# Weight copies issued up to three units ahead, and constant multiplications ahead of TensorE's waits, in a two-block transformer kernel

## The reference, cut to what matters

```python
def first_block(x, ...):              # 1040 tokens
    h = rms_norm(h_res, pre_mix_g); proj = h @ w_in            # q1 q2 k1 k2 v u
    o = diff_attention(q1, q2, k1, k2, v, lam)                 # causal, softmax(q1 k1) - lam softmax(q2 k2)
    y = s5_ssm(u, ...); y = y * sigmoid(gelu(y) @ w_glu + b)   # state space side
    h_res = h_res + rms_norm(concat(o, y) @ w_out)
    h = rms_norm(h_res); f = (silu(h @ w_gate) * (h @ w_up)) @ w_down    # width 2816
    return h_res + rms_norm(f)
def second_block(x, p, ...):
    proj = rms_norm(x) @ w_in                                  # retention q k v gate, RWKV columns
    mixed = concat(retention(...), rwkv7_mix(...))
    x = x + mixed @ w_o
    x = x + (silu(hf @ w_gate) * (hf @ w_up)) @ w_down         # hf = rms_norm(x)
    x = x + (p @ w_ple_up) * sigmoid(rms_norm(x) @ w_ple_gate)
    return rms_norm(x)
```

## Time and profile before

| what | value |
| --- | --- |
| median of 3 runs | 3360.91 us (3358.93 to 3362.32) |
| the profiled execution: its time | 3366.5 us |
| its span, first to last instruction | 3364.7 us |
| PE busy | 3066.1 us (91%) |
| PE weight loads / DVE / ACT / POOL busy | 71% / 45% / 36% / 36% |
| mean granted TensorE clock | 0.950 |

### The profile page before, as it was taken

One profiled execution on the slowest core, in us unless ns is written; L12 is line 12 of the kernel. 1 busy time (PEld: TensorE's weight loads), 2 busy tenths in 40 slices (PEclk: granted clock), 3 DMA queues, 4 the chain that ended last, 5 costly groups with the idle time before them and its releaser, 6 DMA issues.

```text
span 3364.7 us, 48162 instructions
## 1 busy us (share of the span) xinstructions
PE 3066.1 (91%) x19536; PEld 2383.2 (71%) x19536; DVE 1510.8 (45%) x2264; ACT 1225.0 (36%) x1969; POOL 1224.4 (36%) x698
## 2 busy tenths in 40 slices
PE   6997888899998889989999989998999988899997
PEld 4775656666776667777777767776777766788875
DVE  5835552444443441465565453435445554222233
ACT  3111134533433463334444345342444433322233
POOL 5811302232323323334444433424444422344432
PEclk9888789899999989999999999998999989999998
DMA  4344323222222444322222244332222222322231
GB/s 152 117 128 110 101 77 111 93 69 82 74 68 78 138 145 157 105 78 76 80 84 67 85 153 157 118 101 79 73 90 78 79 70 79 121 98 95 93 106 57
DMA packets 158029, 330.01 MB, mean 98 GB/s; under 512 B 34960, under 2 KB 74064, under 8 KB 157808
## 3 DMA queue, kind: packets, MB, share of 16 engines
q1 hardware_dynamic: 104000, 237.86, 22.7%
q10 hardware_dynamic: 53808, 89.07, 7.7%
HBM read 281.89 MB, written 44.97 MB: 97 GB/s over the span
## 4 chain that ended last, share of the span: by engine, by line
PE 77%; DVE 10%; ACT 4%; POOL 3%; issue 2%; DMA 2%; ACTq 1%; SPq 0%; DVEq 0%; POOLq 0%
PE ps L1953 31%; PE ps L1979 13%; PE ps L1991 12%; POOL w_lo L735 2%; PE ps L1804 2%; PE ps L1715 2%; PE ps L1685 1%; DVE acc_dense L2386 1%; PE ps L1725 1%; PE ps L1832 1%; DVE act_lo L2386 1%; ACT w_hi L846 1%; PE ps L2185 1%; DVE turn L2386 1%; PE ps L1892 1%
## 5 line engine op out<-in xcount | busy, mean ns | idle before, releaser
L735 POOL TENSOR_TENSOR w_lo<-w_raw,w_hi 128x1024 fp32r<-128x1024 f32 x408 | 995.1, 2451 | 1695.9 <-ACT w_hi L846 1692.3
L1953 PE MATMUL ps<-act_hi,w_hi 128*128 128x512 f32 x1696 | 700.4, 413 | 36.6 <-POOL w_lo L735 26.6
L1953 PE MATMUL ps<-act_hi,w_lo 128*128 128x512 f32 x1696 | 670.9, 396 | 0.0
L1953 PE MATMUL ps<-act_lo,w_hi 128*128 128x512 f32 x1696 | 670.4, 395 | 0.0
L1953 PEld LDWEIGHTS ps<-act_hi,w_hi 128*128 128x128 f32 x1696 | 323.9, 191 | 128.9 <-issue 48.5
L846 ACT ACTIVATE w_hi<-w_raw 128x1024 fp32r<-128x1024 f32 x378 | 387.1, 1052 | 70.1 <-issue 35.4
L1953 PEld LDWEIGHTS ps<-act_hi,w_lo 128*128 128x128 f32 x1696 | 323.4, 191 | 71.4
L1953 PEld LDWEIGHTS ps<-act_lo,w_hi 128*128 128x128 f32 x1696 | 324.4, 191 | 62.4 <-issue 1.4
L2386 DVE TENSOR_TENSOR acc_dense<-acc_dense,ps 128x512 f32<-128x512 f32 x352 | 241.9, 687 | 247.0 <-PE ps L1979 195.7
L1979 PE MATMUL ps<-w_hi,ffh_hi 128*128 128x512 f32 x704 | 294.0, 418 | 34.3 <-POOL w_lo L735 17.7
L1991 PE MATMUL ps<-w_hi,act_hi 128*128 128x512 f32 x640 | 257.4, 402 | 37.1 <-POOL w_lo L735 22.5
(11 more groups left out here) (380 smaller groups left out, 4346.7 us busy)
## 6 DMA issues: line engine op xcount, KB each, us to landing
w_raw<-weights SPq DMA_DIRECT2D x408, 512.0 KB, 3.5
rw<-rw_t ACTq DMA_DIRECT2D x24, 256.0 KB, 2.4
rw<-lora_t ACTq DMA_DIRECT2D x24, 256.0 KB, 2.0
row<-x ACTq DMA_DIRECT2D x8, 512.0 KB, 4.0
row_dense<-x ACTq DMA_DIRECT2D x8, 512.0 KB, 5.6
row_mix<-res ACTq DMA_DIRECT2D x8, 512.0 KB, 7.5
res<-row_mix ACTq DMA_DIRECT2D x8, 512.0 KB, 4.1
acc_dense<-res ACTq DMA_DIRECT2D x8, 512.0 KB, 6.0
```

The costliest lines, as they stand in the source:

```text
L735: pool.tensor_tensor(w_lo[:, s], raw, w_hi[:, s].bitcast(F32), SUB).then_inc(w_ready, 1)
L1953: mm = pe.matmul(out, ws[w][:, s, P * k:P * k + P], half_acts[h][a][:, k, :], start=(k, w, a) == (0, 0, 0), stop=(k, w, a) == (KT - 1, 1, 0))
```

## The change

Four things change in the code.

1. Weight copies. `W_LOOK` and `weights_by` go. After each event ACT and POOL issue the copies of all units up to three in front of the units already started, as long as the slot was free three events ago (`W_BEHIND` = 4). The start of a unit is no longer looked for.
2. The first three units of phase 1 are copied by POOL itself, right behind the last ones of the opening part; ACT starts with the fourth.
3. `keep_warm(bank, n)` issues `n` matmuls on PE of constant tiles (bf16, 128x128 by 256 columns) into a PSUM bank whose content is not needed at that time. It stands ahead of waits in norms, in late rows of half 1, and at the start of `retention`.
4. At those places the waits are put in another order: those for the PSUM bank come ahead of the constant matmuls, the one for the data behind them. In late rows PE also waits for `s_exp` there.

The constant matmuls are 440 in all: `c` = 1: 40, 10, 10 and 10 behind the last tile; `c` = 3: four times 10; `c` = 4: three times 10 (each of these for both halves); `residual_half`: 10 and 30; `retention`: 10 and 10; late rows: five times 20.

```diff
+    WARM_ROW, WARM_LATE = 10, 20
...
-    W_START, W_AHEAD, W_BEHIND, W_LOOK = len(ORDER), 3, 3, 6
-    EVENTS, begun, ended = {}, [], [W_START] * W_BEHIND
+    W_START, W_AHEAD, W_BEHIND = len(ORDER), 3, 4
+    EVENTS, ended, made_ready = {}, [W_START] * W_BEHIND, [W_START + W_AHEAD]
     def event(side, h, starts, ends):
         ORDER.extend((h, u) for u in starts)
-        begun.append(len(ORDER))
+        assert len(ORDER) <= made_ready[-1]
         ended.append(ended[-1] + len(ends))
-        return side, len(begun) - 1
-    def weights_by(e):
...
+        made_ready.append(min(len(ORDER) + W_AHEAD, ended[-W_BEHIND] + SLOTS))
+        return side, made_ready[-1], ended[-1]
...
-                if pos < W_START:
+                if pos < W_START + W_AHEAD:
                     pool.tensor_tensor(w_hi[:, s], raw, ones[:, 0:1].to_broadcast([P, 1024]), MUL).then_inc(w_hi_made, 1)
...
-        act.wait_ge(w_ready, W_START)
-        round_to(W_START + W_AHEAD)
...
+        def keep_warm(bank, n):
+            for _ in range(n):
+                pe.matmul(ps[:, bank, 0:2 * P], causal[:, 0, :], causal[:, :, :].rearrange("p a n -> p (a n)"), start=True, stop=True)
...
@@ turn_weights
+            if b < len(batches):
+                pe.wait_ge(at_ready, TURNS[v] + b)
             if b == 0:
+                if h and late(h, u):
+                    pe.wait_ge(s_exp, 2 * v + 2)
+                    keep_warm(6, WARM_LATE)
                 pe.wait_ge(a_ready, v + 1)
...
@@ turn_rows
-                    pe.wait_ge(dense_xn, gx + k + 1)
                     if k < 2 and c < 4:
                         pe.wait_ge((mix_kept, None, out_added)[c - 1], 2 * HALF * h + HALF + 2 * k + 2)
                     if k >= 2:
                         pe.wait_ge(dense_ready, gt_ + k - 1)
+                    if k and (c < 4 or k >= 2):
+                        keep_warm(2 * (k % 2), WARM_ROW * (4 if (c, k) == (1, 1) else 1))
+                    pe.wait_ge(dense_xn, gx + k + 1)
...
+            pe.wait_ge(dense_ready, gt_ + HALF - 1)
+            keep_warm(0, WARM_ROW)
             pe.wait_ge(dense_ready, gt_ + HALF)
...
@@ residual_half
-                    pe.wait_ge(xn_ready, g + 1)
                     pe.wait_ge(act_ready, g - 1)
+                    if step == 2:
+                        keep_warm(4 + 2 * (g % 2), WARM_ROW * (3 if h else 1))
+                    pe.wait_ge(xn_ready, g + 1)
...
@@ retention
             pe.wait_ge(tok_done, 4 * HALF * (h + 1))
+            keep_warm(4, WARM_ROW)
             pe.wait_ge(rot_done, 2 * HALF * (h + 1))
```

More of the change, by code:

```diff
@@ L547, in build @@
     ORDER = [(0, u) for u in range(U_V, U_GLU)] + [(0, u) for u in range(U_V)] + [(1, u) for u in range(U_V, U_GLU)] + [(0, U_GLU), (0, U_GLU + 1)]
-    W_START, W_AHEAD, W_BEHIND, W_LOOK = len(ORDER), 3, 3, 6
-    EVENTS, begun, ended = {}, [], [W_START] * W_BEHIND
+    W_START, W_AHEAD, W_BEHIND = len(ORDER), 3, 4
+    EVENTS, ended, made_ready = {}, [W_START] * W_BEHIND, [W_START + W_AHEAD]
     def event(side, h, starts, ends):
         ORDER.extend((h, u) for u in starts)
-        begun.append(len(ORDER))
+        assert len(ORDER) <= made_ready[-1]
         ended.append(ended[-1] + len(ends))
-        return side, len(begun) - 1
-    def weights_by(e):
-        soon = begun[min(e + W_LOOK, len(begun) - 1)]
-        return max(begun[min(e + 1, len(begun) - 1)], min(soon, begun[e] + W_AHEAD, ended[e + 1] + SLOTS))
+        made_ready.append(min(len(ORDER) + W_AHEAD, ended[-W_BEHIND] + SLOTS))
+        return side, made_ready[-1], ended[-1]
     for phase, h, mix, dense, ends in ((1, 1, heads_starts, first_starts, first_ends), (2, 0, mix_starts, first_starts, first_ends),
@@ L573, in build @@
     assert ended[-1] == len(ORDER)
-    assert all(weights_by(e) <= ended[e + W_BEHIND] + SLOTS for e in range(len(begun)))
-    EVENTS = {phase: [(side, weights_by(e), ended[e + W_BEHIND]) for side, e in events] for phase, events in EVENTS.items()}
     AT = {key: pos for pos, key in enumerate(ORDER)}
@@ L1561, in dense_half @@
             yield from dense_norm(5, h)
-        rounded = [W_START]
+        rounded = [W_START + W_AHEAD]
         def round_to(n):
@@ L1568, in round_to @@
                 s = pos % SLOTS
+                if pos == W_START + W_AHEAD:
+                    act.wait_ge(w_hi_made, pos)
                 act.wait_ge(w_landed[s], 16 * (pos // SLOTS + 1))
@@ L1811, in turn_weights @@
             e, batches = attn[h]["e_br"][:, v % 2, 0], key_batches(qi)
+            if b < len(batches):
+                pe.wait_ge(at_ready, TURNS[v] + b)
             if b == 0:
+                if h and late(h, u):
+                    pe.wait_ge(s_exp, 2 * v + 2)
+                    keep_warm(6, WARM_LATE)
                 pe.wait_ge(a_ready, v + 1)
             if b < len(batches):
-                pe.wait_ge(at_ready, TURNS[v] + b)
                 k0, nk = batches[b]
@@ L2050, in residual_half @@
                     g = tiles[step - 2][0]
+                    pe.wait_ge(act_ready, g - 1)
+                    if step == 2:
+                        keep_warm(4 + 2 * (g % 2), WARM_ROW * (3 if h else 1))
                     pe.wait_ge(xn_ready, g + 1)
-                    pe.wait_ge(act_ready, g - 1)
                     for k in range(KT):
```

## The result

The changed kernel takes 3331.39 us (median of 10 runs, 3323.46 to 3352.12), the kernel before 3360.72 beside it (10 runs, 3351.81 to 3363.13). The ratio is 0.9917 (0.99 to 0.9934): 28 us faster, between 22 and 34. The forecast was 3289, 72 us faster, with a range up to 3325. The direction was right, the size was too large by more than twice.

The account below looks back on a forecast made before the run. PE was taken as the bound (91% busy, 77% of the last chain). Terms -11.1 - 61 + 16 - 16 = -72 took the profiled 3366.5 to 3294.5, less 5.6 to the median: 3289 us, range 3262 to 3325.

Parts of the forecast that it names:

- The step that failed: PE's waits for weights after the start: nearly all of 55.1 us go; next late are DVE's and ACT's results.
- POOL is no bottleneck here: Starts of phase 1 and retention: POOL's subtraction is late because ACT's copy is late, queued behind mixing-side waits.
- The copies and the start: Earlier weight copies -61 us (bounds -38 and -76); start of phase 1 -11.1 us (bounds -8 and -13).
- The start: Start of phase 1: 9.8 of PE's 11.7 us gap goes, plus 1.3 for the clock; -11.1 us.
- Refill and clock behind the stalls: Behind PE's 30 other waits for weights: 8.1 us of refilling PE and 13 us of half-clock work would go.
- The price of the constant matmuls: 0.114 us each; 310 lie free in waits, 130 exposed in 13 groups cost +16 us (bounds 12 and 30).
- Their gain: Around norms and late rows, constant matmuls keep PE's clock up: 55% of 28 us, -16 us (bounds 0 and -28).
- the first rival: In norms and late rows the constant matmuls hold no clock, so their gain is 0: 3305 us; chance 0.20.
- Another wait takes the place: Events behind the weights wait for DVE or ACT; gain 49 us instead of 72: 3312 us; chance 0.17.
- The slower rival: ACT's copies wait for transfers not landed, holding up mixing work in its queue: 3377 us at 0.3 each; chance 0.04.

Follow-up runs that it names:

- weights only: Changed kernel with all `keep_warm` calls taken out, weight copies and new order of waits kept; 3328.8 us.
- weights only with POOL behind: Changed kernel without constant matmuls, plus a wait holding POOL's subtractions right behind ACT's `ffh_hi` until DVE has made `ffh_lo`; 3307.3 us.

## Why the prediction was wrong

**The step that failed** is the one on what is late next: "nearly all of these waits should go; what is late next is what the same instructions wait for anyway", and with it "POOL is no bottleneck here". The waits for weights did all go, though not with the leads that the forecast counted (9 to 21 events): worked out from the two rules, 52 units of 375 still have three events, as before, and the others 4 to 31. But it treated POOL's subtraction as work that costs nothing wherever it lies, as long as it is early. It moved 2.4 us instructions onto DVE's, mostly right behind ACT's `ffh_hi`, where DVE's `ffh_lo` and the first additions of a down product are due. The copies and the start were to bring 61 + 11.1 = 72 us; without constant matmuls they brought 28.8 in the rest, and 53.2 with POOL held back. 24 us of the difference is this collision (30 with the constant matmuls; 21 and 34 in the medians), shown by undoing it alone. With it undone, the change gives 3297.2, 8 us from the forecast, but that is partly luck: copies and start are still 19 us short of their 72, and the constant matmuls, forecast to come to nothing, make up for 12 of it.

**The start**, forecast at 11.1, brought about 4. The wait for the transfer of the keys was named and priced at too little: it is 5.4 us in the changed kernel, and behind it PE works at half clock (0.50 in 530.3 to 534.0 us), as it did behind the old gap.

**Refill and clock behind the stalls**, 8.1 + 13 us in the forecast, did not show. They would be time of PE's own work, and in the rest this stays as it was. Columns as in the earlier trace rows; before, then weights only, then weights only with POOL behind:

```profile
516.09:3364.70 2848.61, 2626.52 (x17505) 2062.90 (x17505) 1219.79 (x1737) 1103.54 (x1672) 1052.20 (x586) 0.96 0.29 95
```
```profile
504.70:3324.60 2819.90, 2627.31 (x17505) 2069.15 (x17505) 1224.17 (x1737) 1100.14 (x1669) 1052.05 (x583) 0.96 0.30 96
```
```profile
508.10:3303.50 2795.40, 2621.04 (x17505) 2065.95 (x17505) 1201.78 (x1737) 1100.42 (x1669) 1040.15 (x583) 0.97 0.30 97
```

The same 17505 matmuls take 2626.5, 2627.3 and 2621.0 us. PE's idle time falls from 222.1 to 192.6 and 174.4: with the collision undone, 47.7 of the 66.5 us of waits for weights are carried, 0.72 where the forecast took 0.8, and 5.5 of the 21 us of refill and clock come with it. The new waits, for `acc_dense` above all, have their own clock behind them.

**The price of the constant matmuls** was right: 40 of them take 4.54 us, the last 0.27 of its own, so (4.54 - 0.27) / 39 = 0.109 us apart against 0.114. The cost of the 130 exposed ones was 8 in the one pair of profiles, not 16. Why it is less was not tried; some may lie where PE would have waited for DVE a little later.

**Their gain** had the right sign and was larger. They hold the clock, so the first rival falls, and what the prediction worked out, that groups of ten among transposes would hold nothing, did not come true: with them the mean clock is 0.967 against 0.954, and the norm of half 0 shows it. Before, its tiles 1 and 2:

```profile
597.34 1.97 PE L1933 MATMUL ps<-ident,xn_dense 128*128 128x128 f32 x8 [7.11 <-DVE xn_dense L2393]
602.69 1.97 PE L1933 MATMUL ps<-ident,xn_dense 128*128 128x128 f32 x8 [3.39 <-DVE xn_dense L2393]
```

In the changed kernel the transposes run at full clock, 1.09 us, behind 40 and behind ten:

```profile
580.99 4.54 PE L1627 MATMUL ps<-causal 128*128 128x256 bf16 x40 [2.21 <-ACT acc_dense L842]
586.73 1.09 PE L1940 MATMUL ps<-ident,xn_dense 128*128 128x128 f32 x8 [1.20 <-DVE xn_dense L2405]
588.18 1.27 PE L1627 MATMUL ps<-causal 128*128 128x256 bf16 x10 [0.36 <-DVE act_lo L2398]
592.08 1.09 PE L1940 MATMUL ps<-ident,xn_dense 128*128 128x128 f32 x8 [2.63 <-DVE xn_dense L2405]
```

Whether the transposes themselves count for the clock no run here separates. The norm of the earlier trace rows has 1.09 us for its last three tiles now, and 1.94 in the kernel with the weights only. PE is busy for 27.5 us more in the rest than without them (2654.8 against 2627.3), though the 440 take some 55 (440 x 0.124): its other work is some 27 us shorter, where the forecast took 16. The 55 us fill 33 us of idle time, so some 21 are exposed, where the forecast took 16. As a whole they come to nothing by themselves, as forecast (2848.4 against 2848.6), and to 6 and 12 us in the rest once the weights are early (3 the other way and 10 in the medians).

**The rivals.** "Another wait takes the place" is what happened, but for the larger part not by the mechanism given: the additions were not due then anyway; they were made late. With the collision undone 28.6 us of the wait are left against 15.8 before, and that part may be what this rival described. It was priced at 3312 and given 0.17. The slower rival's mechanism was there, 76.5 us of ACT's waits instead of 11.1; what they cost was not isolated, and making them fewer brought no gain.

## What to carry to other kernels

Before work of POOL is moved, look at which DVE instructions will lie beside it. Here a subtraction of two SBUF tiles and the two steps on `e_br` from SBUF to SBUF took some 2 us longer beside it, and an addition with one operand in PSUM did not. A PE product that alternates between two PSUM banks and waits for DVE has little slack against that. An instruction that is early enough can be held back for free; one wait on the side that has slack was worth more here (34 us) than the change itself (28), though by itself, in the kernel before, it brought nothing. Compare the busy time of an engine whose instructions did not change: here it was the first sign. And a long instruction costs only where somebody waits: 13 long `ffh_lo` before cost PE little.

## What the runs showed of the hardware

DVE's `ffh_lo` of 512 columns takes 0.69 us, and up to 2.8 with a subtraction of POOL beside it; its `e_br` of 912 columns, with one SBUF tile and a column of `small` as inputs, goes from 0.69 to 2.92, and the next one, with two tiles, from 1.17 to 3.14. POOL's subtraction takes 2.35 us alone and 2.75 (8.26 / 3) in that stretch. I had not expected the size of it: the 18 long ones in the changed kernel are 29 us of DVE beyond their 0.69; taking 26 of these away took 30 us out of the rest, idle time and lower clock of PE together.

The lead of a unit's copy has an edge. With three events 52 units cost PE nothing in the changed kernel; with one event for 44 of them it took 158 us longer.
